# A front in another order and one query projection fewer in a hybrid attention layer

## The chip, the cores and the metric

The kernel runs on one core of a Trainium2 chip. The metric is the device time of one execution in microseconds, as the median of several runs; lower is better.

## The reference

The kernel computes one layer of a decoder trunk on x of 512 tokens by 1024 features, in float32:

```
h = rms_norm(x)
q,k,v (8 MoBA heads), q (8 NSA heads), kv (cmp,slc,win), gates = split(h @ w_in)
y_A = moba_attention(...)            # rms-normed q, k; relative bias table
y_B = nsa_attention(...)             # compressed, selected and window branch
x = x + (sigmoid(gA) * (y_A @ w_br_moba) + sigmoid(gB) * (y_B @ w_br_nsa)) @ w_o
x = x + (gelu(conv_a) * conv_b) @ w_down      # conv3 of rms_norm(x) @ w_up
x = x + sigmoid(x @ w_ple_gate) * (p @ w_ple)
```

With 512 tokens each of MoBA's selections and NSA's selected and window branches covers all past keys, so the kernel computes causal attention for them, and a small one over 31 compressed keys for the compressed branch.

## The kernel before

All weights and activations are split into a high part (rounded to fp32r) and a low part (the rest). Each product is three matmuls, high by high, high by low, low by high (`three`, L1400 to L1402). The token axis has NT = 4 tiles of 128, the depth axis KT = 8 tiles of 128. Five engines run programs written out by hand, with semaphores between them; the DMAs are issued by SP, a few at the start by ScalarE.

**The front.** SP loads x, the rows of constants, unit 0's weights in two halves and the first gate's weights. ScalarE and VectorE sum the squares of x. VectorE scales x (L1088) and splits unit 0's weights (L1057 high part, L1064 the low part of even depth tiles, GpSimd the low part of odd ones at L609, after it has built the bias table `rtab`, L601). TensorE turns x (L1417) and, after four of the eight depth tiles, the constants (L1408). ScalarE takes `hTh` out of PSUM (L846), VectorE `hTl` (L1097). Then TensorE projects unit 0, token tile by token tile with the depth inside, the first from the fifth `hTl` on, and runs gate 0. The vectors of unit 0 are turned (L1451) after GpSimd (L655, tiles 0 and 1) and VectorE (tiles 2 and 3) have copied them.

**The units.** A projection unit w brings the columns for one pair of heads. Units 1 to 4 have q, k and v of two MoBA heads (384 columns). Units 5 and 7 have q of two NSA heads and k and v of a group (384). Units 6 and 8 have q alone (128 columns). A unit's work after the projection is a sum of squares, `rstd`, `normalise` (L1150 on VectorE for token tiles 2 and 3, L639 on GpSimd for 0 and 1), the turning of its two or four vectors (`turn_vector`), and `vec_high`, `vec_low`, which take them into `QQ`, `Kh`, `Kl`.

**The attention** is a list of 104 steps, 8 for each of pairs 0 to 3 and 18 for each of pairs 4 to 7. A step takes the scores of one query tile of one head; steps 9 and 18 of the later pairs are those over the compressed keys. `PROJ`, `SPLIT`, `NORM` and `VEC` say at which step a piece of a later unit's work is done: unit 6 is projected in the first 8 steps of pair 4, unit 7 in the last 6 of pair 4 and the first 10 of pair 5, unit 8 in the first 8 of pair 6. Output gates are computed in between. Behind the attention come 184 chunks of weights for the branch products, `w_o`, the feed-forward part and the last gate.

## Time and profile before

| | us |
|---|---|
| median of 3 runs (1001.71 to 1003.32) | 1003.06 |
| the profiled execution, its own time | 1001.79 |
| its span in the trace | 1000.0 |
| TensorE busy | 914.0 |
| VectorE busy | 484.8 |
| ScalarE busy | 405.2 |
| GpSimd busy | 381.3 |

The trace is of one execution; times in it count from the start of its span. Matmuls are pipelined, so their records overlap: a matmul's duration is longer than the distance between two starts, and it is this distance that counts in a full stream. PE is TensorE, PEld its weight loads, DVE VectorE, ACT ScalarE, POOL GpSimd. The granted clock is 1.00 for 2.4 GHz and 0.50 for 1.2 GHz.

### The profile page before, as it was taken

To read this page: it belongs to the slowest core of one execution; us is meant where nothing else is said; L and a number is where in the kernel's file an instruction comes from. 1 tells how busy PE (TensorE), PEld (TensorE's weight loads), DVE (VectorE), ACT (ScalarE), POOL (GpSimd) and SP (SyncE) were. 2 spreads that over 40 slices of the span, in tenths; PEclk is the share of its full clock that TensorE was granted. 3 is DMA by queue.
4 is the path that set the end of the run, shared out by engine and by line. 5 is a ranking of instruction groups with operands and counts; after the bars stand their busy time and mean duration, and the time that the engine had idled before them with its cause. 6 is when DMAs were issued, how large, how long until landed. Compare 5 with 4: busy or idle time off the path is not lost.

```text
span 1000.0 us, 13463 instructions
## 1 busy us (share of the span) xinstructions
PE 914.0 (91%) x4621; PEld 779.4 (78%) x4621; DVE 484.8 (48%) x1179; ACT 405.2 (41%) x857; POOL 381.3 (38%) x364
## 2 busy tenths in 40 slices
PE   3998798787999799999989999999999999999988
PEld 2897688686878687877767778888888888888866
DVE  6516666767675767786441343344433343000032
ACT  3221454444454444554434344444444443232320
POOL 6333312312120301025544566444454445464540
PEclk9998899999999899999999999999999999999999
DMA  5655213214122111333554425333333333332222
GB/s 158 153 138 137 63 47 81 54 38 111 43 73 77 32 53 57 113 127 123 179 199 132 116 95 147 98 93 95 95 95 108 104 95 95 96 99 91 85 94 86
DMA packets 99046, 99.34 MB, mean 99 GB/s; under 512 B 16068, under 2 KB 73380, under 8 KB 98980
## 3 DMA queue, kind: packets, MB, share of 16 engines
q1 hardware_dynamic: 98927, 98.48, 33.7%
q8 instruction: 39, 0.64, 0.3%
q14 instruction: 27, 0.22, 0.1%
q10 hardware_dynamic: 53, 0.01, 0.0%
HBM read 87.58 MB, written 10.88 MB: 98 GB/s over the span
## 4 chain that ended last, share of the span: by engine, by line
PE 78%; DVE 13%; issue 4%; ACT 3%; DMA 1%; POOL 0%; SPq 0%; POOLq 0%; ACTq 0%; DVEq 0%
PE banks L1400 24%; PE banks L1402 23%; PE banks L1401 23%; DVE plain_arena L1150 2%; PE banks L1533 2%; DVE plain_arena L1178 1%; PE banks L1451 1%; DVE split_arena L1064 1%; DVE split_arena L1223 1%; PE banks L1516 1%; PE banks L1515 1%; PE banks L1475 1%; ACT split_arena L821 1%; DVE split_arena L1057 1%; DMA plain_arena<-in_x_dram 1%
## 5 line engine op out<-in xcount | busy, mean ns | idle before, releaser
L1400 PE MATMUL banks<-split_arena 128*128 128x512 f32 (+4 forms) x1256 | 479.1, 381 | 15.5 <-POOL split_arena L645 4.1
L1401 PE MATMUL banks<-split_arena 128*128 128x512 f32 (+4 forms) x1256 | 467.0, 372 | 0.0
L1402 PE MATMUL banks<-split_arena 128*128 128x512 f32 (+4 forms) x1256 | 466.9, 372 | 0.0
L645 POOL TENSOR_TENSOR split_arena<-plain_arena,split_arena 128x512 fp32r<-128x512 f32 x184 | 238.7, 1310 | 248.7 <-ACT split_arena L837 248.7
L1400 PEld LDWEIGHTS banks<-split_arena 128*128 128x128 f32 x1256 | 240.2, 191 | 59.3 <-issue 13.1
L1402 PEld LDWEIGHTS banks<-split_arena 128*128 128x128 f32 x1256 | 239.7, 191 | 36.2
L1401 PEld LDWEIGHTS banks<-split_arena 128*128 128x128 f32 x1256 | 240.4, 191 | 32.5
L837 ACT ACTIVATE split_arena<-plain_arena 128x512 fp32r<-128x512 f32 x184 | 113.3, 628 | 196.4 <-PE banks L1402 189.4
L809 ACT ACTIVATE plain_arena<-plain_arena 128x128 f32<-128x128 f32 (+1 forms) x96 | 53.9, 562 | 137.3 <-DVE plain_arena L1178 137.3
L1361 DVE SCALAR_TENSOR_TENSOR plain_arena<-banks,plain_arena 128x511 f32<-128x511 f32 x44 | 32.7, 743 | 135.4 <-ACT plain_arena L938 135.4
L613 POOL TENSOR_TENSOR split_arena<-plain_arena,split_arena 128x512 fp32r<-128x512 f32 x16 | 25.7, 1606 | 146.1 <-ACT split_arena L894 135.1
L609 POOL TENSOR_TENSOR split_arena<-plain_arena,split_arena 128x384 fp32r<-128x384 f32 (+2 forms) x36 | 36.3, 1019 | 106.4 <-ACT split_arena L752 92.9
L1178 DVE CUSTOM_DVE_ANT_0 plain_arena<-banks,plain_arena 128x128 f32<-128x128 f32 (+1 forms) x96 | 46.7, 486 | 43.0 <-PE banks L1516 42.5
L1223 DVE TENSOR_TENSOR split_arena<-banks,split_arena 128x128 fp32r<-128x128 f32 (+1 forms) x96 | 46.9, 489 | 36.1 <-ACT split_arena L821 35.9
L1533 PE MATMUL banks<-plain_arena 128*128 128x128 f32 x240 | 43.7, 281 | 9.7 <-DVE split_arena L1223 5.1
L1451 PE MATMUL banks<-plain_arena 128*128 128x128 f32 x128 | 22.2, 307 | 27.6 <-DVE plain_arena L1150 19.3
L1379 DVE TENSOR_TENSOR plain_arena<-banks,plain_arena 128x512 f32<-128x512 f32 x8 | 5.0, 683 | 86.4 <-PE banks L1402 86.4
L1451 PEld LDWEIGHTS banks<-plain_arena 128*128 128x128 f32 x128 | 16.2, 157 | 32.9 <-issue 21.5
L821 ACT ACTIVATE split_arena<-banks 128x128 fp32r<-128x128 f32 (+1 forms) x96 | 40.1, 418 | 2.2 <-PE banks L1533 1.2
L639 POOL TENSOR_TENSOR plain_arena<-plain_arena 128x256 f32<-128x256 f32 (+1 forms) x32 | 18.3, 603 | 58.6 <-DVE plain_arena L1048 29.8
L1533 PEld LDWEIGHTS banks<-plain_arena 128*128 128x128 f32 x240 | 28.9, 142 | 13.9 <-issue 12.4
L938 ACT ACTIVATE plain_arena<-banks,plain_arena 128x512 f32<-128x512 f32 x44 | 30.6, 777 | 22.3 <-PE banks L1402 22.3
(156 smaller groups left out, 843.2 us busy)
## 6 DMA issues: line engine op xcount, KB each, us to landing
plain_arena<-in_w_up_dram SPq DMA_DIRECT2D x88, 256.0 KB, 3.2
plain_arena<-in_w_down_dram SPq DMA_DIRECT2D x44, 256.0 KB, 2.6
plain_arena<-in_w_in_dram SPq DMA_DIRECT2D x18, 512.0 KB, 4.2
plain_arena<-in_w_in_dram SPq DMA_DIRECT2D x32, 192.0 KB, 3.6
plain_arena<-in_x_dram SPq DMA_DIRECT2D x8, 512.0 KB, 4.6
gates<-plain_arena SPq DMA_DIRECT2D x16, 256.0 KB, 2.3
plain_arena<-skew SPq DMA_DIRECT2D x16, 256.0 KB, 3.7
plain_arena<-in_w_in_dram SPq DMA_DIRECT2D x64, 64.0 KB, 2.1
```

Of the source, the lines that this page charges most:

```text
L609: pool.tensor_tensor(Wl[:, kt, 0:c], raw[:, kt, 0:c], Wh[:, kt, 0:c].bitcast(F32), ALU.subtract).then_inc(w_lo[1], 1)
L645: pool.tensor_tensor(W2l[:, c % RING, :], raw2[:, c % RING, :], W2h[:, c % RING, :].bitcast(F32), ALU.subtract).then_inc(w2_lo, 1)
L809: nc.scalar.activation(prob[:, t % 4, 0:nk], prob[:, t % 4, 0:nk], ACT.Exp, bias=mneg[:, t % 4:t % 4 + 1], scale=-1.0, accum_out=rsum[:, t ...
L821: nc.scalar.activation(PTh[:, s["u"] % 2, 0:i + 1, P * i:P * (i + 1)], PS[:, 4 + t % 2, 0:P * (i + 1)].rearrange("p (j q) -> p j q", j=i + ...
L837: nc.scalar.activation(W2h[:, c % RING, :], raw2[:, c % RING, :], ACT.Copy).then_inc(w2_hi, 1)
L1178: nc.vector.tensor_tensor_reduce(out=prob[:, t % 4, 0:nk], in0=PS[:, 2 + t % 2, 0:nk], in1=strip[:, n % 2, e, S - nk:S], scale=1.0, scalar ...
L1223: nc.vector.tensor_tensor(PTl[:, s["u"] % 2, 0:i + 1, P * i:P * (i + 1)], PS[:, 4 + t % 2, 0:P * (i + 1)].rearrange("p (j q) -> p j q", j= ...
L1400: nc.tensor.matmul(o, ah, bh, start=first, stop=False)
L1401: nc.tensor.matmul(o, ah, bl, start=False, stop=False)
L1402: return nc.tensor.matmul(o, al, bh, start=False, stop=last)
L1451: ins = nc.tensor.transpose(PS[:, vec_bank(w, x), P * tt:P * (tt + 1)], qn[:, tt, x, :], ident)
L1533: ins = nc.tensor.transpose(PS[:, 4 + t % 2, P * j:P * (j + 1)], prob[:, t % 4, P * j:P * (j + 1)], ident)
```

## The change

In the front, TensorE runs 20 matmuls of the constant `ones` by itself, turns the constants, runs 8 more of them, and only then turns x. ScalarE takes the high part of all of unit 0's weights before it copies the turned constants; GpSimd takes all low parts, under a semaphore of their own (`w0_lo`). VectorE no longer splits unit 0; it scales x in two halves of the features. GpSimd builds the bias table after unit 0's and gate 0's low parts instead of before. SP issues the second gate's load ahead of the skew table's spill. Unit 0 is projected with the depth outermost for two token tiles at a time, in four banks of PSUM. In the later units, unit 6 now brings the queries of pair 5 and of pair 7 (256 columns, four vectors), and unit 8 is gone; pair 7's queries stay in a third slot of `QQ`. The diff, cut to its core; the rest are places where 6 and 8 were excepted and uses of the new slot:

```diff
-        return 2 * P + 24 if w == 0 else (P if w in (6, 8) else CW)
+        return {0: 2 * P + 24, 6: 2 * P}.get(w, CW)
     def udmas(w):
         return {0: 0, 5: 3, 7: 3}.get(w, 1)
     def nvec(w):
-        return 2 if w in (6, 8) else 4
-
-    W_UNITS = 9
+        return 4
+
+    W_UNITS = 8
...
-        QQ = R[:, 24576:26624].rearrange("p (s e q) -> p s e q", s=2, e=2)
+        QQ = [R[:, o:o + 1024].rearrange("p (e q) -> p e q", e=2) for o in (24576, 25600, 37760)]
...
-            eng.wait_ge(w_lo[kt % 2], KT // 2 * w + kt // 2 + 1)
+            if w == 0:
+                eng.wait_ge(w0_lo, kt + 1)
+            else:
+                eng.wait_ge(w_lo[kt % 2], KT // 2 * (w - 1) + kt // 2 + 1)
...
+            if w == 0:
+                return (0, 1, 4, 5)[tt]
             return 6 if w <= 2 and tt % 2 and (w, tt) != (2, 3) else 0
...
+        def qslot(n):
+
+            return 2 if n == NPAIR - 1 else n % 2
+
         def vec_dst(w, x):
             n = w - 1
+            if w == 6:
+                return "q", qslot(5 if x < 2 else 7), x % 2
             if x < 2:
-                return "q", n % 2, x
+                return "q", qslot(n), x
             return ("k", n % 2, x - 2) if n < 4 else ("k", (n - 4) // 2, x - 2)
...
-                        sp.dma_start(raw[:, kt, 0:P], win[kt][:, C_NQ + n * P:C_NQ + (n + 1) * P]).then_inc(raw_in[kt], 16)
-                        if n % 2 == 0:
-
+                        if w == 6:
+                            src = win[kt][:, C_NQ:C_NQ + 512].rearrange("p (a b c) -> p a b c", a=2, b=2)[:, :, 1, :]
+                            sp.dma_start(raw[:, kt, 0:2 * P].rearrange("p (a c) -> p a c", a=2), src).then_inc(raw_in[kt], 16)
+                        else:
+                            sp.dma_start(raw[:, kt, 0:P], win[kt][:, C_NQ + n * P:C_NQ + (n + 1) * P]).then_inc(raw_in[kt], 16)
                             g = n // 2
...
+            load_gate_weights(1)
             sp.wait_ge(rtab_done, 1)
             for c0, part in ((0, rtab), (S, masked)):
                 width = part.shape[1]
                 sp.dma_start(skew_d[:, :, c0:c0 + width], part.unsqueeze(1).broadcast_to([16, NREP, width])).then_inc(skew_out, 16)
-            load_gate_weights(1)
...
-            pool.wait_ge(rbt_in, 16)
-            pool.wait_ge(pool_const, 12)
-
-            for b, (lo, hi) in enumerate(bucket_edges()):
-                ins = pool.tensor_scalar(rtab[:, S - hi:S - lo], rbt[:, b:b + 1].broadcast_to([16, hi - lo]), -1.0, None, ALU.mult)
-            ins.then_inc(rtab_done, 1)
-
             def split_unit(w, kts):
...
-            split_unit(0, range(KT))
+            for kt in range(KT):
+                pool.wait_ge(w_hi, kt + 1)
+                pool.tensor_tensor(Wl[:, kt, 0:ucols(0)], raw[:, kt, 0:ucols(0)], Wh[:, kt, 0:ucols(0)].bitcast(F32), ALU.subtract).then_inc(w0_lo, 1)
             split_gate(0)
+            pool.wait_ge(rbt_in, 16)
+            pool.wait_ge(pool_const, 12)
+
+            for b, (lo, hi) in enumerate(bucket_edges()):
+                ins = pool.tensor_scalar(rtab[:, S - hi:S - lo], rbt[:, b:b + 1].broadcast_to([16, hi - lo]), -1.0, None, ALU.mult)
+            ins.then_inc(rtab_done, 1)
             pool.wait_ge(cst_done, 1)
...
+            w_high(0, range(KT))
             act.wait_ge(cst_turned, 3)
             nc.scalar.activation(cst[:, 0:CONVW + P + 4], PS[:, 0, 0:CONVW + P + 4], ACT.Copy).then_inc(cst_done, 1)
...
-            for tt in range(NT):
-                nc.vector.tensor_scalar(xnat[:, tt, :], xnat[:, tt, :], st[:, 80 + tt:81 + tt], None, ALU.mult).then_inc(h_nat, 1)
-            split_unit(0, range(KT))
+            for half in range(2):
+                for tt in range(NT):
+                    part = xnat[:, tt, half * 512:(half + 1) * 512]
+                    nc.vector.tensor_scalar(part, part, st[:, 80 + tt:81 + tt], None, ALU.mult).then_inc(h_nat, 1)
             dve.wait_ge(cst_done, 1)
             dve.wait_ge(pool_const, 4)
-
-            for c in (GQ, GQ + 2):
-                link(nc.vector.tensor_scalar(cst[:, c:c + 1], cst[:, c:c + 1], -(DH ** -0.5), None, ALU.mult))
             for kt in range(KT):
                 dve.wait_ge(hT_hi, kt + 1)
                 nc.vector.scalar_tensor_tensor(out=hTl[:, kt, :], in0=PS[:, turn_bank(kt), :], scalar=cst[:, kt:kt + 1],
                                                in1=hTh[:, kt, :].bitcast(F32), op0=ALU.mult, op1=ALU.subtract).then_inc(hT_lo, 1)
+            for c in (GQ, GQ + 2):
+                link(nc.vector.tensor_scalar(cst[:, c:c + 1], cst[:, c:c + 1], -(DH ** -0.5), None, ALU.mult))
             gate_high(0)
...
-                if k == 4:
-                    rsqrt(rq[:, 0:16], ss[:, 0:16], 1.0 / DH, 16, done=rstd_done)
-                else:
-                    rsqrt(rq[:, 20:28], ss[:, 0:8], 1.0 / DH, 8)
-                    nc.vector.tensor_copy(rq[:, 0:16].rearrange("p (t v) -> p t v", t=NT)[:, :, 0:2],
-                                          rq[:, 20:28].rearrange("p (t v) -> p t v", t=NT)).then_inc(rstd_done, 1)
+                rsqrt(rq[:, 0:16], ss[:, 0:16], 1.0 / DH, 16, done=rstd_done)
...
-                    pe.wait_ge(h_nat, tt + 1)
+                    pe.wait_ge(h_nat, NT * (kt // 4) + tt + 1)
...
-                    if w == 0:
-                        pe.wait_ge(hT_lo, 5)
...
-            for kt in range(4):
+            def warm(count):
+
+                pe.wait_ge(pool_const, 4)
+                for _ in range(count):
+                    nc.tensor.matmul(PS[:, 7, 0:P], ones, ones, start=True, stop=True)
+
+            def project_first():
+
+                pe.wait_ge(cst_done, 1)
+                for pair in ((0, 1), (2, 3)):
+                    for kt in range(KT):
+                        wait_weights(pe, 0, kt)
+                        pe.wait_ge(hT_lo, kt + 1)
+                        for tt in pair:
+                            t_ = slice(P * tt, P * (tt + 1))
+                            ins = three(PS[:, proj_bank(0, tt), 0:ucols(0)], hTh[:, kt, t_], hTl[:, kt, t_], Wh[:, kt, 0:ucols(0)], Wl[:, kt, 0:ucols(0)],
+                                        kt == 0, kt == KT - 1)
+                            if kt == KT - 1:
+                                ins.then_inc(proj_filled, 1)
+                        if pair[1] == NT - 1 and kt < KT - 1:
+                            ins.then_inc(w_used, 1)
+
+            warm(20)
+            turn_consts()
+            warm(8)
+            for kt in range(KT):
                 turn_input(kt)
-            turn_consts()
-            for kt in range(4, KT):
-                turn_input(kt)
-            for tt in range(NT):
-                project(0, tt)
+            project_first()
             gate(0)
```

## Rows read from the trace of the kernel before

**Rows 1.** The page, part 4: the chain that ended last, by engine.
```profile
PE 78%; DVE 13%; issue 4%; ACT 3%; DMA 1%; POOL 0%; SPq 0%; POOLq 0%; ACTq 0%; DVEq 0%
```

**Rows 2.** Windows, TensorE: stretch, length, busy (x), granted clock, DMA share, GB/s.
```profile
13.00:14.00 1.00, 0.83 (x2) 1.00 0.84 188
14.00:15.00 1.00, 0.62 (x3) 1.00 0.04 8
...
22.00:23.00 1.00, 0.00 (x0) 0.84 0.00 0
...
29.00:30.00 1.00, 1.00 (x8) 0.75 1.06 291
```

**Rows 3.** The chain in order of time, first projection and pair 4: start, us, what.
```profile
25.75 0.60 PE banks L1400
...
27.05 0.23 PE banks L1401
...
35.12 0.13 PE banks L1401
...
251.87 0.11 PE banks L1401
...
254.86 0.12 PE banks L1402
```

**Rows 4.** Timeline of VectorE: start, us, instruction, forms, count.
```profile
14.80 0.51 DVE L1057 CAST split_arena<-plain_arena 128x280 fp32r<-128x280 f32 x2
...
16.38 3.18 DVE L1057 CAST split_arena<-plain_arena 128x280 fp32r<-128x280 f32 x2
...
22.31 5.36 DVE L1097 SCALAR_TENSOR_TENSOR split_arena<-banks,plain_arena,split_arena 128x512 fp32r<-128x512 f32 x8
...
273.71 0.89 DVE L1150 TENSOR_TENSOR plain_arena<-plain_arena 128x128 f32<-128x128 f32 x4
...
341.22 3.31 DVE L1150 TENSOR_TENSOR plain_arena<-plain_arena 128x256 f32<-128x256 f32 x4
```

**Rows 5.** Timeline of GpSimd in the front, columns as before.
```profile
9.10 9.51 POOL L601 TENSOR_SCALAR plain_arena<-plain_arena 16x1 f32<-16x1 f32 x32 [4.34 <-DMA plain_arena<-in_rel_bias_dram]
18.58 2.34 POOL L609 TENSOR_TENSOR split_arena<-plain_arena,split_arena 128x280 fp32r<-128x280 f32 x3
...
28.34 1.79 POOL L613 TENSOR_TENSOR split_arena<-plain_arena,split_arena 128x512 fp32r<-128x512 f32 x1 [5.69 <-DVE split_arena L1075]
31.35 0.74 POOL L655 COPY plain_arena<-plain_arena 128x256 f32<-128x256 f32 x2 [1.22 <-ACT plain_arena L747]
```

**Rows 6.** Windows between compressed-key steps: busy (x) of PE, PEld, DVE, ACT, POOL; clock; DMA.
```profile
326.72:361.50 34.78, 28.30 (x157) 23.61 (x156) 26.29 (x84) 17.61 (x48) 10.75 (x14) 0.90 0.11 32
361.50:389.43 27.93, 27.93 (x193) 25.11 (x193) 16.09 (x61) 12.29 (x36) 1.79 (x1) 1.00 0.26 75
389.43:415.69 26.26, 22.50 (x135) 18.95 (x133) 21.65 (x78) 12.62 (x32) 4.17 (x6) 1.00 0.13 41
415.69:435.65 19.96, 19.48 (x110) 16.10 (x109) 15.22 (x58) 10.04 (x28) 1.78 (x1) 1.00 0.64 206
435.65:458.34 22.69, 19.71 (x114) 16.21 (x112) 18.65 (x58) 14.28 (x36) 9.43 (x7) 1.00 0.25 87
```

**Rows 7.** Groups by form, ScalarE: xcount | busy us, mean ns | idle before.
```profile
L752 ACT ACTIVATE split_arena<-plain_arena 128x384 fp32r<-128x384 f32 x32 | 14.2, 511 | 0.0
...
L846 ACT ACTIVATE split_arena<-banks,plain_arena 128x512 fp32r<-128x512 f32 x8 | 4.9, 693 | 1.9 <-PE banks L1417 1.9
```

**Rows 8.** Timeline of TensorE, after the first gate and in the feed-forward part.
```profile
45.28 1.03 PE L1451 MATMUL banks<-plain_arena 128*128 128x128 f32 x8
...
48.31 0.42 PE L1400 MATMUL banks<-split_arena 128*128 128x384 f32 x1
...
578.60 1.16 PE L1639 MATMUL banks<-plain_arena 128*128 128x128 f32 x8 [1.58 <-DVE plain_arena L1345]
```

**Rows 9.** Line L1417, window 13 to 20.2 us: duration ns min/median/max, first and last start.
```profile
L1417 PEld LDWEIGHTS banks<-plain_arena x24: 141/230/231, 13.0 to 19.5; 128*128 128x128 f32 x24
```

More of the change, by code:

```diff
@@ L288, in layer @@
         cst_done = sem("cst_done")
+        w0_lo = sem("w0_lo")
         w_hi, w_lo = sem("w_hi"), [sem("w_lo_even"), sem("w_lo_odd")]
@@ L685, in _ @@
                     normalise(NORM[t])
-                if t in VALUES and VALUES[t] not in (6, 8):
+                if t in VALUES and VALUES[t] != 6:
                     v_low(VALUES[t])
@@ L744, in take_proj @@
                     act.wait_ge(norm_done, w)
-                    if w - 1 not in (6, 8):
-                        act.wait_ge(v_lo, min(w - 1, 5) if w - 1 < 7 else 6)
+                    if w < 7:
+                        act.wait_ge(v_lo, w - 1)
                 nc.scalar.activation(qkv[:, tt, 0:ucols(w)], PS[:, proj_bank(w, tt), 0:ucols(w)], ACT.Copy).then_inc(qkv_done, 1)
@@ L902, in _ @@
                     w_high(*SPLIT[t])
-                if t in VALUES and VALUES[t] not in (6, 8):
+                if t in VALUES and VALUES[t] != 6:
                     v_high(VALUES[t])
@@ L1514, in scores @@
                     nk = P * (i + 1)
[L1515 to L1516 removed]
+                    nc.tensor.matmul(o[:, 0:nk], QQ[qslot(n)][:, e, P * i:P * (i + 1)], Kh[:, ks, ke, 0:nk], start=True, stop=False)
+                    ins = nc.tensor.matmul(o[:, 0:nk], QQ[qslot(n)][:, e, P * i:P * (i + 1)], Kl[:, ks, ke, 0:nk], start=False, stop=True)
                 ins.then_inc(score, 1)
```

18 lines of the change are left out of this document (8 added, 10 removed).

## The prediction

> **What bounds the kernel now.** I read the page's chain first: TensorE holds 78% of it and VectorE 13% [rows 1]. So time is won in two ways only: by taking matmuls out of TensorE's stream, or by closing stretches in which it waits. The windows show such a stretch at the start: the transfers are over by 14 us (share 0.84 in 13:14, 0.04 in 14:15) [rows 2], yet the first projection begins at 25.75 us [rows 3]. VectorE's timeline shows what lies between: unit 0's weights are split from 14.80 us on, with one pair of casts that took 3.18 us where the same pair took 0.51 before, and only at 22.31 us does it come to `hTl` (L1097), for which the projection waits [rows 4]. GpSimd was building the bias table then, from 9.10 us for 9.51 [rows 5]. Last, the windows from one compressed-key step (the 9th and the 18th of each pair of heads 4 to 7) to the next show what a projection unit costs inside the attention [rows 6].
>
> **The front, part by part.** *Weights of unit 0* go from VectorE to ScalarE and GpSimd. A 384-column cast takes ScalarE 0.51 us [rows 7]; I take 0.4 for 280 columns. The second half of the weights lands between 12 and 14 us, I take 13.0, so the last four casts end at 14.6 us. The copy of the turned constants now stands behind them in ScalarE's order, some 0.4 us: 15.0. That is the new wait, and all of `hTh` and `hTl` are queued behind it; the constants themselves are turned earlier. *x* is scaled in halves: the whole is done at 14.8 us as before, the first half over a microsecond earlier, so turning x lies beside ScalarE's casts. The first `hTh` takes 0.7 us [rows 7]: 15.7. Then `hTl` paces with 5.36/8 = 0.67 us [rows 4]. TensorE's last turn (kt 7) needs the second `hTl`, at 17.1 us, and takes some 0.6 us: the projection starts at 17.7 us instead of 25.75.
>
> *Depth-outermost.* A 280-column matmul advances by 0.23 us at the low clock level and 0.13 at the high one [rows 3] (0.127, from the end point below). A depth step of two tiles is six of them, 0.76 us, longer than the 0.67 between two `hTl`: TensorE isn't starved. GpSimd's low parts of the weights take 2.34/3 = 0.78 us each [rows 5], kt 7 done by 19 us, wanted at 23. The 96 matmuls take 12.2 us and end at 29.9. Before, the gate followed the last one 24 x 0.228 = 5.5 us ahead of 45.28 [rows 8], at 39.8. Gain 9.9 us. Of this 1.6 is clock: before, the first 3.7 us of the projection ran at 1.2 GHz (15 matmuls x 0.106).
>
> *Constant matmuls.* 28 of them run from about 1.5 us, when TensorE has nothing else before 13 us. Their nearest row, the products with `ones` at 578.60 us, has 8 passes for 4 products in 1.16 us [rows 8]: 0.25 us each at 2.4 GHz, at most twice that at 1.2. So 20 are over at 6.5 to 11.5 us and the 8 behind the constants take 2 to 4 us, over before 15. Their cost is nothing: they lie beside the loads and ScalarE's casts, and if that cover were gone it would be the 2 to 4 us of the last 8. What they buy is the high level. The granted clock fell within 22:23, about 3 us after TensorE had gone idle, and rose within 29:30 [rows 2]. In the new order I find no idle stretch over 1.5 us ahead of the projection and price it at the high level.
>
> The Trainium skill (TensorE: Matmul & The Clock Gate, Part 4: PE-mode transpose) says that work in the transpose mode doesn't count towards opening the full clock. By it the constant matmuls would be forgotten while x is turned, and the projection would start at 1.2 GHz, 1.6 to 2.9 us more. The trace of before speaks against it: from 13.0 us TensorE did almost nothing but transposes, and their weight loads went from 231 to 141 ns within them [rows 9].
>
> *GpSimd's bias table* moves behind unit 0's weights and the gate's. The gate's high part is there at about 22.2 us (`hTl` ends at 21.1, then two small instructions and one cast), its low part takes 1.79, then the table 9.51: 33.5 us. Four copies follow, 0.74 for two: 35.0 us [rows 5]. Turning unit 0's vectors waits for them, and TensorE comes to it when the gate ends, 29.9 + 5.5 = 35.4 us. That is a cover of 0.4 us. Behind the copies GpSimd splits the odd weights of unit 1, 4 x 0.78 x 384/280 = 4.3 us: 39.3, wanted at 35.4 + 3.0 [rows 8] + 3.6 = 42.0. VectorE's casts for unit 1 fall beside the table this time, as unit 0's did before. I charge 1.0 us for this corner; the bounds are 0 and 4. On SP the spill of the skew table waits for the table, with the loads of unit 1 and of gate 1 ahead of it; the strips that read it are wanted tens of microseconds later. Front: -9.9 + 1.0 = **-8.9 us**. The later waits of the front hang on TensorE's own progress and move along.
>
> **The merged unit.** Units 6 and 8 are 96 matmuls of 128 columns each. Such a matmul advances by 0.11 us (piece at 251.87), and one of 256 columns by 0.12 (254.86) [rows 3]. Halving the count saves TensorE 96 x 0.11 = 10.6 us. What of it reaches the path is read from [rows 6], where like steps stand beside each other. Nine steps with unit 8's projection take 27.93 us, the same nine a pair later without one 19.96: -7.97 (not 10.6, since the softmax chain shows through). The nine with unit 8's normalisation and two vectors take 26.26, without 22.69: -3.57. Against it, pair 4 gets two more vectors to turn, eight transposes, 1.0 us [rows 8], and a normalisation 256 wide. On VectorE four 128-wide instructions took 0.89 us, four 256-wide ones beside GpSimd 3.31 [rows 4]. Unit 6 has no values for GpSimd to split, so only the first of the four meet it: I take 2.2 us, +1.3. With 0.2 for wider matmuls and copies: -7.97 - 3.57 + 1.0 + 1.3 + 0.2 = **-9.0 us**. Bounds: with the transposes alone -10.3. If the merged unit behaves like unit 7, the window 326.72:361.50 applies: 34.78 less 2.1 (two steps of its projection, 12 matmuls at 0.17) less 22.69 = 10.0 for a four-vector unit against 3.57 for a two-vector one, 6.4 more: -5.1. I stay near the first end, since unit 7's values are what unit 6 lacks. The third query slot takes a wait away and adds none; eight dropped SP issues, four ScalarE copies and one VectorE rsqrt chain are in the windows already.
>
> **Sum.** 1001.79 (the profiled run, whose span is 1000.0) - 8.9 - 9.0 = 983.9: **984 us**. The median shown is 1.3 above that run, so 985 would be as fair.
>
> **Rivals.** (a) *The four-vector stall.* Merging gives 5.1: 1001.8 - 8.9 - 5.1 = 988. For it: in unit 7's window the clock fell to a mean of 0.90 [rows 6]. Against: no value split. (b) *The front meets GpSimd.* Table, copies and odd weights are 3 us later than summed, weights or clock cost another 1: 1001.8 - 4.9 - 9.0 = 988. For it: the 0.4 us of cover and the 3.18 us pair [rows 4]. Against: most of VectorE's work then is ahead of need. The Trainium skill has a rule that would sharpen it (SBUF — State Buffer, Who interferes with whom): VectorE's casts and GpSimd's instructions block each other for whole instructions rather than slow each other a little. (c) *Both*: 992. (d) *Better than summed*: no collision, no widening, one fall of the clock fewer: 979 to 981. (e) *Slower than before*: the table, now ahead of unit 0's copies, holds TensorE back so long that 17.9 us are gone. It decides from the point where it takes 9.5 + 0.4 + 1.0 + 17.9 = 29 us; at 32 the kernel is at 1005. The worst collision seen is 3.2 us for a pair, so this needs six such. (f) *Nothing happens in front*, since x or weights bind: 1001.8 - 9.0 = 993. Against: VectorE had x and all weights in hand by 16.38 us at the latest, without a wait [rows 4].
>
> **Numbers.** The forecast (981 to 987) 0.45, (a) 0.17, (b) 0.17, (c) 0.06, (d) 0.08, (f) 0.03, within 0.2% 0.01, (e) 0.03. The range goes from 979 to 992 and holds the first five. Within 0.2% (2 us) is about what a measurement of this kernel can't tell from no change. Faster 0.96, same 0.01, slower 0.03.
>
> **What would show it.** Right: the first 280-column matmul at 17 to 18.5 us with 0.127 between starts; the gate's first at 29 to 31; no wait of the vectors' turning for L655; all of the attention some 9 us earlier at its start; the nine steps after pair 5 in 20 to 21 us, not 27.93; pair 4's stretch 2 to 3 us longer. Wrong: a projection that starts at 0.23 us spacing, VectorE casts of over 1 us between 24 and 34 us with TensorE waiting for them, or a pair 4 stretch over 5 us longer.

## The result, and the profile after

The changed kernel takes 994.37 us (median of 4 runs, 993.43 to 994.84) against 1003.19 us (median of 4 runs, 1001.71 to 1006.77): a ratio of 0.9903, 95% interval 0.9886 to 0.992. It is faster by 8.8 us, where 17.9 were summed. The profiled execution took 993.43 us, its span is 991.6 us.

First the page of the changed kernel, part 4, the chain by engine. It answers to [rows 1]: TensorE has the same share, VectorE one per cent less.

```profile
PE 78%; DVE 12%; issue 4%; ACT 4%; DMA 1%; POOL 0%; SPq 0%; POOLq 0%; ACTq 0%; DVEq 0%
```

TensorE's timeline in the front (start, us, instruction, forms, count, idle before). L1577 are the constant matmuls, L1428 turns x, the 280-column matmuls are the first projection, the first 512-column one is the gate, L1460 turns the vectors of unit 0.

```profile
1.53 7.61 PE L1577 MATMUL banks<-plain_arena 128*128 128x128 f32 x40 [1.53 <-POOL plain_arena L603]
9.99 0.56 PE L1419 MATMUL banks<-plain_arena 98*128 98x98 f32 x3 [0.85 <-DMA plain_arena<-in_conv_w_dram]
10.49 2.05 PE L1577 MATMUL banks<-plain_arena 128*128 128x128 f32 x16
...
17.01 5.05 PE L1428 MATMUL banks<-plain_arena 128*128 128x128 f32 x29 [0.58 <-DVE plain_arena L1106]
21.82 0.38 PE L1411 MATMUL banks<-split_arena 128*128 128x280 f32 x1
...
34.04 0.29 PE L1413 MATMUL banks<-split_arena 128*128 128x280 f32 x1
34.17 0.39 PE L1411 MATMUL banks<-split_arena 128*128 128x512 f32 x1
...
39.63 1.04 PE L1460 MATMUL banks<-plain_arena 128*128 128x128 f32 x8
43.77 1.26 PE L1460 MATMUL banks<-plain_arena 128*128 128x128 f32 x8 [3.10 <-DVE plain_arena L1130]
```

The projection starts at 21.82 us instead of 25.75 [rows 3], and runs through at 0.13 us from one matmul to the next. But it was to start at 17.7. TensorE turns x late, and its idle time names L1106, VectorE's scaling of x. Behind the gate it waits 3.10 us for L1130. VectorE's timeline says why in both places:

```profile
11.57 0.16 DVE L1062 TENSOR_TENSOR plain_arena<-plain_arena 128x4 f32<-128x4 f32 x1
11.76 0.71 DVE L1063 SCALAR_TENSOR_TENSOR plain_arena<-plain_arena 128x4 f32<-128x4 f32 x1
12.51 0.70 DVE L1064 SCALAR_TENSOR_TENSOR plain_arena<-plain_arena 128x4 f32<-128x4 f32 x1
13.24 6.35 DVE L1106 TENSOR_SCALAR plain_arena<-plain_arena 128x512 f32<-128x512 f32 x8
19.51 5.35 DVE L1111 SCALAR_TENSOR_TENSOR split_arena<-banks,plain_arena,split_arena 128x512 fp32r<-128x512 f32 x8
...
34.42 4.84 DVE L1121 COPY plain_arena<-plain_arena 128x256 f32<-128x256 f32 x4 [1.56 <-ACT plain_arena L762]
...
274.84 2.90 DVE L1161 TENSOR_TENSOR plain_arena<-plain_arena 128x256 f32<-128x256 f32 x4
```

And GpSimd's, to be laid beside it:

```profile
11.67 6.84 POOL L658 TENSOR_TENSOR split_arena<-plain_arena,split_arena 128x280 fp32r<-128x280 f32 x8 [6.91 <-ACT split_arena L767]
25.91 1.80 POOL L620 TENSOR_TENSOR split_arena<-plain_arena,split_arena 128x512 fp32r<-128x512 f32 x1 [7.40 <-DVE split_arena L1091]
27.68 7.94 POOL L664 TENSOR_SCALAR plain_arena<-plain_arena 16x1 f32<-16x1 f32 x32
35.58 1.52 POOL L670 COPY plain_arena<-plain_arena 128x256 f32<-128x256 f32 x4
```

GpSimd begins to subtract unit 0's low parts at 11.67 us. From that moment an instruction of VectorE on 128x4 values takes 0.71 us instead of 0.16, and the scaling of x takes 6.35 us. The four copies of the vectors (34.42 to 39.26 us) lie beside the end of the bias table, GpSimd's own copies and its first weights of unit 1, and take 4.84 us.

Windows over the stretches that stand in [rows 2], and one behind: busy (x) of the engines, clock, DMA. The clock falls at the end of 17:18, behind TensorE's short waits for x, stands at 0.50 in 18:21 and is back at 1.00 in 22:23. So x is turned mostly at the low level, and the projection that begins at 21.82 us is not. It falls again in 45:46, behind the wait for L1130.

```profile
17.00:18.00 1.00, 0.99 (x8) 1.00 (x9) 1.00 (x2) 0.56 (x1) 1.00 (x2) 0.92 0.00 0
18.00:21.00 3.00, 3.00 (x16) 2.89 (x15) 3.00 (x6) 2.65 (x5) 0.51 (x1) 0.50 0.00 0
22.00:23.00 1.00, 1.00 (x10) 1.00 (x9) 1.00 (x3) 0.93 (x2) 0.00 (x0) 1.00 0.00 0
29.00:30.00 1.00, 1.00 (x10) 1.00 (x9) 0.02 (x1) 0.00 (x0) 1.00 (x7) 1.00 1.21 291
45.00:46.00 1.00, 1.00 (x6) 1.00 (x5) 0.92 (x2) 0.98 (x3) 0.00 (x0) 0.57 0.06 16
```

Windows from one compressed-key step to the next, as in [rows 6]; the first row is pair 4's stretch, which ends unit 6 (31.14 us before).

```profile
268.73:303.10 34.37, 30.43 (x169) 26.87 (x168) 28.94 (x85) 17.87 (x44) 10.04 (x10) 0.90 0.11 32
...
365.78:385.76 19.98, 19.49 (x109) 15.97 (x108) 15.35 (x58) 10.04 (x28) 1.79 (x1) 1.00 0.36 104
385.76:407.33 21.57, 19.61 (x116) 16.50 (x114) 16.49 (x58) 11.47 (x30) 3.19 (x2) 1.00 0.16 50
```

27.93 us have become 19.98, and 26.26 have become 21.57. So what unit 8 cost is gone, and pair 4's stretch is 3.2 us longer. What came in its place shows best in a table of leads: how much earlier than before an attention step starts (the start of VectorE's bias instruction on the scores; steps counted from 0 over the whole attention). "From x" is the lead at step 0 counted from the end of ScalarE's last sum of squares instead of from the start of the span; why, is said below the table. "Spread" is the lowest and highest run.

| kernel | lead at step 0 | from x | 26 | 50 | 103 | span | median (spread), runs | ratio, 95% interval |
|---|---|---|---|---|---|---|---|---|
| before: start of the step | 103.96 | 94.23 | 217.42 | 301.61 | 458.34 | 1000.0 | | |
| changed | +1.96 | +1.97 | +1.63 | -4.06 | +8.31 | 991.6 | 994.37 (993.43 to 994.84), 4 | 0.9903, 0.9886 to 0.992 |
| 1 merge only | -0.20 | +0.46 | -0.08 | -7.29 | +5.57 | 995.1 | 997.18 (995.42 to 998.41), 6 | 0.9931, 0.9909 to 0.9952 |
| 2 front only | +0.90 | +2.15 | -0.16 | -0.16 | -0.69 | 1003.6 | 1002.92 (998.42 to 1005.64), 12 | 0.9981, 0.9962 to 1.0 |
| 3 GpSimd after x | +5.64 | +5.64 | +4.87 | -0.81 | +11.01 | 988.2 | 990.8 (989.85 to 992.72), 6 | 0.9868, 0.9847 to 0.989 |
| 4 table late | +5.96 | +6.05 | +4.64 | -1.04 | +11.88 | 992.0 | 992.78 (991.25 to 993.77), 5 | 0.9891, 0.9872 to 0.9909 |
| 5 both | +8.64 | +9.45 | +7.82 | +2.07 | +14.46 | 985.3 | 987.05 (986.91 to 987.41), 4 | 0.983, 0.9805 to 0.9855 |
| 6 changed, no constant matmuls | +0.95 | +1.95 | -0.09 | -5.77 | +7.12 | 993.3 | 995.78 (994.39 to 999.3), 6 | 0.9928, 0.9908 to 0.9948 |
| 7 = 5 + gate waits | +8.71 | +9.49 | +7.14 | +2.51 | +15.02 | 984.4 | 986.69 (983.61 to 987.4), 5 | 0.9828, 0.9808 to 0.9848 |
| 8 = 5 + halves | +9.11 | +10.11 | +7.66 | -0.08 | +12.25 | 987.3 | 989.04 (987.89 to 990.4), 5 | 0.9854, 0.9833 to 0.9875 |
| 9 = 7 + unit 6 on GpSimd | +9.21 | +10.21 | +7.66 | +5.21 | +18.27 | 983.4 | 984.2 (983.95 to 985.21), 4 | 0.9802, 0.9781 to 0.9823 |
| 10 = 7, depth innermost | +7.50 | +8.55 | +7.44 | +1.28 | +13.73 | 987.5 | 989.29 (988.3 to 990.22), 4 | 0.9851, 0.9825 to 0.9876 |
| 11 = 9 + unit 7 on GpSimd | +9.25 | +10.29 | +8.05 | +6.16 | +18.11 | 983.5 | 987.69 (985.58 to 989.59), 5 | 0.9831, 0.9808 to 0.9854 |
| 12 = 9, no constant matmuls | +8.71 | +8.77 | +8.60 | +6.04 | +18.41 | 982.3 | 986.12 (984.13 to 989.33), 5 | 0.9825, 0.98 to 0.9849 |

Each lead comes from one profiled execution. One thing in it is no edit's doing: the last rows of x land early in some of them and about a microsecond later in others. ScalarE's last sum of squares waits for them, as here in the kernel before and in run 9:

```profile
8.58 1.06 ACT L734 ACTIVATE split_arena<-plain_arena 128x1024 fp32r<-128x1024 f32 x1 [1.04 <-DMA plain_arena<-in_x_dram]
```

```profile
9.58 1.06 ACT L754 ACTIVATE split_arena<-plain_arena 128x1024 fp32r<-128x1024 f32 x1 [2.05 <-DMA plain_arena<-in_x_dram]
```

Its result is out at 9.73 to 9.82 us before, in the changed kernel and in runs 3, 4 and 12, and at 10.39 to 10.98 in the others; the column "from x" takes this out. What is left of chance shows in runs 5, 7, 8, 9 and 11, whose programs are the same up to step 0: +9.45 to +10.29. A single difference below about 0.8 us at step 0 shows nothing by itself.

Read the row "changed" from left to right. The front is worth 1.96 us where attention starts. Between steps 26 and 50 (the splits, projection, normalisation and vectors of the merged unit) 5.69 us are lost; from 50 to 103, where unit 8 used to be, 12.37 are won.

### The profile page after: what moved, and what is told of

It reads as the page before. It is cut to its first block, busy times and chain, and to the rows that moved or that the text cites. A ratio compares the mean times of both kernels' runs of the same rounds, so it can differ in the third digit from the quotient of the medians.

```text
span 991.6 us, 13260 instructions
## 1 busy us (share of the span) xinstructions
PE 913.8 (92%) x4581; PEld 779.1 (79%) x4581; DVE 485.4 (49%) x1145; ACT 405.8 (41%) x849; POOL 381.8 (38%) x360
## 4 chain that ended last, share of the span: by engine, by line
PE 78%; DVE 12%; issue 4%; ACT 4%; DMA 1%; POOL 0%; SPq 0%; POOLq 0%; ACTq 0%; DVEq 0%
PE banks L1411 24%; PE banks L1413 23%; PE banks L1412 23%; DVE plain_arena L1161 2%; PE banks L1542 2%; PE banks L1460 1%; DVE plain_arena L1189 1%; DVE split_arena L1080 1%; DVE split_arena L1234 1%; PE banks L1525 1%; PE banks L1524 1%; ACT split_arena L836 1%; PE banks L1484 1%; DMA plain_arena<-in_x_dram 1%; ACT plain_arena L824 1%
## 5 line engine op out<-in xcount | busy, mean ns | idle before, releaser
L1411 PE MATMUL banks<-split_arena 128*128 128x512 f32 (+4 forms) x1224 | 471.3, 385 | 15.7 <-POOL split_arena L652 4.1
L1413 PE MATMUL banks<-split_arena 128*128 128x512 f32 (+4 forms) x1224 | 459.1, 375 | 0.0
L1412 PE MATMUL banks<-split_arena 128*128 128x512 f32 (+4 forms) x1224 | 458.6, 375 | 0.0
L1411 PEld LDWEIGHTS banks<-split_arena 128*128 128x128 f32 x1224 | 234.6, 192 | 58.8 <-issue 12.4
L1413 PEld LDWEIGHTS banks<-split_arena 128*128 128x128 f32 x1224 | 233.4, 191 | 36.3
L1412 PEld LDWEIGHTS banks<-split_arena 128*128 128x128 f32 x1224 | 234.5, 192 | 32.7
L616 POOL TENSOR_TENSOR split_arena<-plain_arena,split_arena 128x384 fp32r<-128x384 f32 (+1 forms) x28 | 31.3, 1127 | 100.7 <-ACT split_arena L767 91.8
L1460 PE MATMUL banks<-plain_arena 128*128 128x128 f32 x128 | 22.6, 311 | 29.0 <-DVE plain_arena L1161 19.8
L1460 PEld LDWEIGHTS banks<-plain_arena 128*128 128x128 f32 x128 | 16.5, 159 | 34.4 <-issue 22.0
L762 ACT ACTIVATE plain_arena<-banks 128x384 f32<-128x384 f32 (+2 forms) x32 | 14.8, 463 | 51.6 <-PE banks L1413 42.0
```

The costliest lines, as they stand in the source:

```text
L1411: nc.tensor.matmul(o, ah, bh, start=first, stop=False)
L1412: nc.tensor.matmul(o, ah, bl, start=False, stop=False)
L1413: return nc.tensor.matmul(o, al, bh, start=False, stop=last)
L1460: ins = nc.tensor.transpose(PS[:, vec_bank(w, x), P * tt:P * (tt + 1)], qn[:, tt, x, :], ident)
```

## The experiments

### 1 and 2: one part alone

Run 1 is the kernel before with the merge; run 2 has the new front and units 6 and 8 apart.

> The kernel before with the merged query units alone. If the two halves of the change add up as the two traces say (first compressed-key step of pair 4 0.8 us later and that of pair 7 8.3 us earlier, 1.6 us ahead just before unit 6 begins to cost), this run is 6 to 7 us faster than before, and its nine steps after pair 5 take about 20 us. If the merge paid only because the front had relieved VectorE and GpSimd, it is less than 4 us faster.

> The changed front with units 6 and 8 apart. By the traces the front is worth 1.5 to 2.5 us: the first projection begins at 21.8 us and not at 25.75, but the first attention step only 2 us earlier. The rival is that the front is worth nothing (within 0.5 us), since the lead of 2 us shrinks again before pair 4.

The ratios say -6.9 us and -1.9 us, together 8.8, where the changed kernel's ratio says -9.7. Run 2's interval reaches 1.0 and its runs spread over 7 us, so its total alone doesn't show a gain; its front, counted from x, starts attention 2.15 us earlier, like the changed kernel's 1.97. Nothing here points to the two parts meeting, and both fell short of the forecast, the front by more. From step 50 to 103 the merge alone wins 12.86; from step 26 to 50 it loses 7.21, of which 1.6 stand at steps 30 to 32 behind a fall of the clock that the changed kernel does not have there.

### 3, 4 and 5: GpSimd out of VectorE's way

```diff
 # 3: GpSimd's low parts of unit 0 start when x is scaled
+pool.wait_ge(h_nat, 2 * NT)
 for kt in range(KT):
     pool.wait_ge(w_hi, kt + 1)
     pool.tensor_tensor(Wl[:, kt, ...], ...)
 # 4: the bias table moves from before the copies of unit 0's vectors to behind
 #    GpSimd's second share of the compressed inputs; the stores of the skew
 #    table on SP go behind load_gate_weights(2)
 # 5: 3 and 4
```

> The changed kernel, with GpSimd's low parts of unit 0 started only after VectorE has scaled x. Theory: these subtractions held up VectorE (eight half tiles in 6.35 us, the last two rsqrt instructions 0.7 us instead of 0.16). Then here the eight take 2.8 to 3.3 us, the projection begins at 17.5 to 18.5 us and ends at 30 to 31. Rival: the halved instructions or ScalarE's casts slow VectorE; then the eight still take over 5 us. At the attention's start I expect at most 1 to 2 us of it, if the bias table's place is the next limit: VectorE's copies and casts for unit 1 stay beside the table.

> The changed kernel with one move: GpSimd builds the bias table (8 us) only after it has subtracted the second set of compressed inputs, so not beside VectorE's four copies of the first unit's vectors; the stores that need the table go behind the gate weights in SP's queue. GpSimd's subtractions stay where the change put them, beside VectorE's scaling of x. Theory (the table beside the copies is the second loss of the front, and independent of the first): the four copies fall from 4.84 to below 2 us, TensorE's stall at the vectors of unit 0 from 3.37 to about 1.2 us, the clock does not fall at 45 us, the first attention step comes 3.5 to 4 us earlier, and the time is 990 to 991.5 us. Rival (the table costs wherever it stands, beside later work of VectorE): the stall moves behind the copies and the time stays at 993.5 to 994.5 us.

> As the run before, and the bias table built after the compressed keys' inputs, where GpSimd is idle (its small input lies in another place, and the skew table is spilled later). Theory: with the table away VectorE's four copies take 1.7 us instead of 4.84, its part of turning unit 0 is not late (2.1 us), the clock does not fall at 45 us (1.7 us), and the 4 us of the run before come through: attention starts 6 to 8 us earlier than in the changed kernel, 987 us. Rival: another wait in the stretch from 48 to 100 us absorbs it, under 3 us faster than the changed kernel.

Run 3, VectorE's timeline:

```profile
11.75 0.16 DVE L1064 SCALAR_TENSOR_TENSOR plain_arena<-plain_arena 128x4 f32<-128x4 f32 x1
12.14 3.26 DVE L1107 TENSOR_SCALAR plain_arena<-plain_arena 128x512 f32<-128x512 f32 x8
15.78 5.36 DVE L1112 SCALAR_TENSOR_TENSOR split_arena<-banks,plain_arena,split_arena 128x512 fp32r<-128x512 f32 x8 [0.38 <-ACT split_arena L863]
...
30.78 4.80 DVE L1122 COPY plain_arena<-plain_arena 128x256 f32<-128x256 f32 x4 [1.39 <-ACT plain_arena L763]
```

The small instructions are back at 0.16 us, x is scaled in 3.26 us, `hTl` starts at 15.78 us (predicted: 15.7), and TensorE's first 280-column matmul at 17.66 (predicted: 17.7). The copies still lie beside the end of the table and what follows it (4.80). Lead at step 0: +3.68 over the changed kernel; at most 1 to 2 us had been expected.

Run 4, VectorE's copies and TensorE's turning of the vectors, one line from either timeline:

```profile
34.11 0.90 DVE L1121 COPY plain_arena<-plain_arena 128x256 f32<-128x256 f32 x4 [1.14 <-ACT plain_arena L762]
```

```profile
41.33 1.26 PE L1460 MATMUL banks<-plain_arena 128*128 128x128 f32 x8 [0.97 <-DVE plain_arena L1130]
```

4.84 us have become 0.90, TensorE's wait 0.97 instead of 3.10, and the clock does not fall at 45 us. Lead at step 0: +4.00 over the changed kernel, as expected, and +3.57 at step 103. The time, though, fell by less than 2 us, and the rival "it costs wherever it stands" seems to have won. It has not: the lead is lost behind the attention, where nothing was changed. Windows of run 4:

```profile
504.00:512.00 8.00, 6.57 (x21) 5.59 (x22) 4.97 (x7) 2.30 (x4) 3.36 (x2) 0.57 0.63 202
562.00:570.00 8.00, 7.74 (x28) 6.59 (x29) 4.13 (x17) 1.60 (x3) 1.28 (x1) 0.57 0.52 172
961.00:969.00 8.00, 6.50 (x16) 5.14 (x17) 4.46 (x6) 0.02 (x1) 1.26 (x1) 0.57 0.70 244
```

The same places in the changed kernel:

```profile
508.00:516.00 8.00, 7.00 (x28) 5.97 (x29) 4.87 (x6) 3.73 (x7) 4.15 (x3) 0.79 0.64 207
566.00:574.00 8.00, 6.43 (x32) 4.85 (x30) 5.15 (x17) 3.21 (x6) 1.79 (x2) 1.00 0.46 151
962.00:970.00 8.00, 6.40 (x22) 5.20 (x23) 4.56 (x6) 0.11 (x1) 1.26 (x1) 0.79 0.76 244
```

At each of them TensorE has a short wait and then runs for a while at 1.2 GHz; a mean of 0.57 over 8 us is 6.9 us at that level, 0.79 is 3.4, 1.00 none. Run 4 has some 14 us more of it in these three windows, and its span is 3.9 us longer than its lead at step 103 says (11.88 against 8.0). The program behind step 103 is the same in both, so small edits are judged by the lead at the next marks rather than by the total. That the low-clock time is all of the 3.9 us is not shown.

Run 5 has both: +8.64 at step 0. Counted from x the gains over the changed kernel are 3.67 and 4.08 alone and 7.48 together, so they add to within 0.3 us. **The front was forecast to be worth 8.9 us; without the two meetings it was worth 8.6, or 9.45 counted from x.** The copies take 1.19 us.

### 6 and 12: what the constant matmuls bring

```diff
-warm(20)
 turn_consts()
-warm(8)
```

> The changed kernel without the 28 constant matmuls (20 ahead of the turning of the constants, 8 behind it); nothing else is changed. Theory (the turning of x raises the clock by itself and the granted clock of the first projection does not come from the constant matmuls): the first projection still advances by about 0.13 us per matmul from its second half on at the latest, the loss is 0 to 1.5 us, 994 to 996 us. Rival (the constant matmuls carry the clock over the first projection): its 96 matmuls run at 0.22 us instead of 0.127 us each for most of its length, the first gate starts 5 to 9 us later than 34.2 us, and the time is 999 to 1003 us.

> The version of 984.2 us without the 28 constant matmuls. Theory (the clock rises from the turning of x alone about 3 to 7 us after it begins, as in the run without them on the changed kernel): now that the projection starts at 18.3 instead of 21.8 us, its first matmuls fall into the low level, until about 21 us, and the loss at the start of attention is 1 to 2 us, 985 to 986.5 us. Rival (with the projection earlier the constant matmuls carry it): the low level lasts over half of the projection, 5 us or more lost. Rival of the other side: no loss, 984 us.

By the plain leads they are worth 1.01 us at step 0 on the changed kernel and 0.50 on the best version. Both are distorted by x, which landed a microsecond late in run 6 and early in run 12. Counted from x the changed kernel loses nothing without them (1.97 against 1.95), and the best version 1.44 us (10.21 against 8.77). That is more than chance: from the start of x's scaling to the first 280-column matmul it is 6.58 us in run 12, and 5.04 to 5.31 in the five runs that have the same front and the constant matmuls. TensorE's timeline of run 12:

```profile
12.84 6.19 PE L1433 MATMUL banks<-plain_arena 128*128 128x128 f32 x32 [2.00 <-DVE plain_arena L1111]
18.79 0.38 PE L1416 MATMUL banks<-split_arena 128*128 128x280 f32 x1
```

and of run 9, which has them:

```profile
13.77 4.75 PE L1433 MATMUL banks<-plain_arena 128*128 128x128 f32 x32 [0.42 <-DVE plain_arena L1111]
18.28 0.37 PE L1416 MATMUL banks<-split_arena 128*128 128x280 f32 x1
```

Run 12 begins to turn x 0.93 us earlier and starts the projection 0.51 us later: that is the 1.44 us. It turns x at the low level at first (6.19 us instead of 4.75); its weight loads for that take 0.23 us up to 17.4 us and 0.14 behind it, though the profile's row of the granted clock says 1.00 from 12.8 us on. The projection runs at the full clock: the turning itself has raised it. So the first theory stands, and the loss of 1.4 us is the expected 1 to 2. On the changed kernel nothing is lost: x is turned mostly at the low level there with the constant matmuls too (0.50 in 18:21). The gain does not last: at step 26 run 12 is 0.94 us ahead of run 9 by the plain lead, and at step 103 0.14. Its total spreads over 5 us and settles nothing by itself.

### 7, 8, 9 and 11: the merged unit

In run 5 the 5.75 us lost between steps 26 and 50 lie in four places, by the same leads: 1.71 while unit 6's weights are split (steps 26 to 30), 0.74 with its projection (30 to 41), 2.31 at its normalisation (41 to 42), 0.99 with its vectors.

```diff
 # 7: GpSimd's gate subtraction at unit 6 starts when VectorE has normalised
+if t > n6 and not gated: gated.append(j); pool.wait_ge(norm_dve, 7)
 split_gate(j + 1)
 # 8: VectorE normalises two of unit 6's vectors, and the others a step later
-if t - 1 in NORM: normalise(NORM[t - 1])
+if t - 1 in NORM: normalise(6, 0, 2) if NORM[t - 1] == 6 else normalise(NORM[t - 1])
+if t - 2 in NORM and NORM[t - 2] == 6: normalise(6, 2, 4)
 # 9: unit 6's low parts all on GpSimd (11: unit 7's too)
-if kt % 2:
+if kt % 2 or w == 6:
```

> The version with both GpSimd moves (987.05 us) and one wait more: at unit 6 GpSimd's subtraction for the gate weights (1.53 us) starts only when VectorE has normalised its half of unit 6. Theory (VectorE's 2.90 us for four 128x256 instructions is its meeting with GpSimd's subtraction): they take 1.5 to 2.0 us, TensorE's stall of 4.27 us at 267.9 us falls to 3.1 to 3.4 us, and the time is 986 us. Rival (256 columns cost what they cost): 2.90 us and 4.27 us stay, and the time is 987 us.

> The version with both GpSimd moves (987.05 us), and VectorE normalises the two vectors for pair 5 of unit 6 where it now does all four, and the two for pair 7 one attention step later (four instructions of 128x128 twice instead of four of 128x256 once). Theory (the merge's extra stall is VectorE doing twice the work in one place with TensorE waiting behind it): the first half takes 0.9 to 1.5 us, TensorE's stall of 4.27 us at 267.9 us falls to about 2 to 2.8 us as before the change, little of it comes back a step later, and the time is 985 to 986 us. Rival (the work only moves to the next step, where TensorE waits for it too): one stall of 2.3 us and a new one of 1.5 to 2 us, and the time is 987 us.

VectorE's timeline of run 7, then of run 8, at the normalisation:

```profile
269.34 1.83 DVE L1166 TENSOR_TENSOR plain_arena<-plain_arena 128x256 f32<-128x256 f32 x4
```

```profile
270.28 2.37 DVE L1161 TENSOR_TENSOR plain_arena<-plain_arena 128x128 f32<-128x128 f32 x4
```

In run 7 the four instructions take 1.83 us instead of 2.90 once GpSimd's subtraction is out of the way; TensorE loses 1.24 us there instead of 2.31. Run 8 has half the work in the first place and still takes 2.37 us, where the same form took 0.89 before the change [rows 4]. GpSimd is what differs: before, its own half of the normalisation was over (272.17 + 1.47 = 273.64 us) when VectorE's began at 273.71. One of run 8's four, of 128x128, bears most of it:

```profile
271.10 1.35 DVE L1161 TENSOR_TENSOR plain_arena<-plain_arena 128x128 f32<-128x128 f32 x1
```

Run 7's last three, clear of GpSimd, take 1.08 us, so four of 128x256 would take about 1.4 (an estimate from that). Then the meetings cost the same at either width, 2.37 - 0.89 = 1.5 and 2.90 - 1.4 = 1.5, and the width about 0.5. Run 8 pays for the second half too: by the leads it loses 0.5 us less than run 5 at the normalisation and 1.0 more in the steps behind. It ends 2 us behind run 5, but most of that is not the edit's: 1.5 us are lost between steps 30 and 32, before the normalisation, where the clock fell (a mean of 0.66 in 231:236) and run 5's did not.

> The version with both GpSimd moves and the gate's wait at unit 6 (986.69 us), and the low parts of unit 6's weights are all subtracted by GpSimd, where VectorE takes every other one (0.86 us of VectorE in each of four steps beside GpSimd's 0.72, where 128 columns took 0.29 before the change). Theory (attention steps 27 to 30 lengthen by 0.4 to 0.6 us each because VectorE's and ScalarE's splits of unit 6 are twice as wide): with VectorE's part gone the lead over the kernel before falls between steps 26 and 30 by 0 to 0.6 us instead of 1.7, and the time is 985.0 to 986.0 us. Rival (ScalarE's 0.72 instead of 0.51 us sets the steps, or GpSimd's longer work slows VectorE as much): the lead still falls by 1.4 us or more, and the time is 986.5 to 987 us or above.

The splits, VectorE's timeline of run 5 with two of its four halves:

```profile
223.45 0.87 DVE L1081 TENSOR_TENSOR split_arena<-plain_arena,split_arena 128x256 fp32r<-128x256 f32 x1
...
227.81 0.86 DVE L1081 TENSOR_TENSOR split_arena<-plain_arena,split_arena 128x256 fp32r<-128x256 f32 x1
```

In run 9 these lines are gone, GpSimd does all eight; the first four:

```profile
221.63 2.98 POOL L616 TENSOR_TENSOR split_arena<-plain_arena,split_arena 128x256 fp32r<-128x256 f32 x4
```

From step 26 to 30 the lead now rises by 0.40 us where run 7 loses 1.73: the whole cost of the splits in these steps was VectorE's share. Both are measured in the same stretch, so this is shown. Part of it is again a meeting: in run 5 GpSimd's own subtraction ran from 227.66 to 228.38 us, and VectorE's of 227.81 ended only at 228.67. With 984.2 us run 9 is the fastest here, 10 us below the changed kernel. That it lies 0.2 from the forecast is chance, since it got there by edits that the forecast did not have.

> The version of 984.2 us (both GpSimd moves, the gate's wait at unit 6, unit 6's low parts on GpSimd), with unit 7's low parts on GpSimd alone too (384 columns, 1.14 us each, two in a step). Theory (VectorE leads the chain of every step in which weights are split, and GpSimd has time): the lead rises by 0.5 to 1.5 us over the steps in which unit 7 is split, 983 to 984 us. Rival (in these steps TensorE has its projection to do and waits for nobody): the lead does not change, 984 to 984.5 us; or GpSimd is late for the projection of unit 7 and the time is 985 us or more.

The lead at step 50 rose by 0.95 us, inside what was expected, but nothing of it is left at step 103, and the median is 3.5 us higher, with no run as fast as run 9's slowest. A gain is not shown. The expectation's reason for a slower kernel, GpSimd late for unit 7's projection, doesn't fit a lead that had risen by step 50; where the 3.5 us are lost stays open.

### 10: depth innermost

```diff
-for pair in ((0, 1), (2, 3)):
+for pair in ((0,), (1,), (2,), (3,)):
     for kt in range(KT):
```

> The version with both GpSimd moves and the gate's wait at unit 6 (986.69 us), with the first unit's projection turned back from depth-outermost in two pairs of token tiles to one token tile after the other; banks and everything else stay. Theory (worked from the trace: a pair of depth tile takes TensorE 0.8 us and VectorE delivers one hTl in 0.67 us, so depth-outermost never waits, while one token tile alone takes 0.4 us for each depth tile and is paced by the 0.67 us): the projection ends 1 us later, the first attention step 1 us later, 987.5 to 988 us. Rival (something behind the projection sets the start of attention in any case): no change, 986.3 to 987 us. Rival of the other side (the order is the main gain of the front): 3 us later or more.

TensorE's timeline of run 10 has gaps in the first token tile, where it waits for `hTl`:

```profile
20.73 0.29 PE L1418 MATMUL banks<-split_arena 128*128 128x280 f32 x1
21.11 0.40 PE L1416 MATMUL banks<-split_arena 128*128 128x280 f32 x1
...
21.47 0.29 PE L1418 MATMUL banks<-split_arena 128*128 128x280 f32 x1
```

Between the start of the last matmul of one depth step and the first of the next lie 0.38 us instead of 0.13, and a depth step takes 0.74 us (20.73 to 21.47). The loss at step 0 is 1.21 us, or 0.94 counted from x, near the 1 us worked out. The total lost 2.6, but this is not the order's price: at step 26 the lead is again run 7's (7.44 against 7.14), and between steps 30 and 32 1.5 us are lost where run 10's clock fell (a mean of 0.66 in 233:238) and run 7's did not. So the new order is worth about 1 us where attention starts, and a lasting gain is not shown.

## Why the prediction was wrong

**The sign was right and the size was half: two meetings of VectorE with GpSimd and the price of the wider splits were missing from the sum.** The first step that failed is the sentence "the whole is done at 14.8 us as before": the scaling of x. It is done at 19.6. The prediction took this duration over from the kernel before and did not ask what GpSimd would be doing beside it. Before the change GpSimd was building its table there, and VectorE's small instructions took 0.16 us and the whole scaling 2.74 beside it; now it is eight wide subtractions, which the change itself brings forward to 11.67 us. All of the chain behind it (`hTh`, `hTl`, the projection) is the sum's, 3.8 to 4.3 us late: the first `hTl` 19.51 for 15.7, the first matmul 21.82 for 17.7, the gate 34.17 for 29.9. Run 3 takes that one meeting away and gets 15.78 and 17.66.

**The corner of table, copies and odd weights** was charged 1.0 us with bounds of 0 and 4. It costs 4.00 (run 4), the upper end: the second step that failed. GpSimd itself was in time: the table took 7.94 us and not 9.51, its copies were done at 37.1, before TensorE came at 39.6. Late was VectorE: the prediction found its casts for unit 1 ahead of need and did not look at the four copies, with casts and the copies of the compressed inputs (L1130) queued behind them. Rival (b) named the engines and the 4 us, but put the delay on GpSimd. Together the two account for the front: 9.9 - 3.7 - 4.0 = 2.2 us, measured 1.96.

**Depth-outermost, ScalarE's casts, the clock.** The projection was never starved, and its matmuls advanced by 0.129 us (12.22 us over 95), 0.127 predicted. The casts were done at 14.4 us (14.6 predicted), the copied constants at 14.7 (15.0). The constant matmuls cost nothing, but they did not do what they were priced for. TensorE waited 1.81 us for x where the prediction found "no idle stretch over 1.5 us", and the granted clock was 0.50 from 18 to 21 us; it was back before the projection began at 21.82, but not for the prediction's reason, since the projection has the high level without the constant matmuls too (runs 6 and 12). So the price held by luck. Where x comes in time they save some 1.4 us of its turning. With both meetings out of the way the front was worth 8.64 us in run 5 against 8.9, or 9.45 counted from x.

**The merge.** Its removals were summed at 7.97 + 3.57 = 11.5 us; 12.4 were won. The vectors (1.0) cost 0.99. Normalisation was put at +1.3 and cost 2.3: the term assumed that one of the four instructions lies beside GpSimd, and the gate's subtraction of 1.53 us met a second one, for about 1.1 us (2.90 against run 7's 1.83). "0.2 for wider matmuls and copies" is the worst mis-sized and the third step that failed: 1.7 for the splits and 0.7 for the projection, 2.4 in all. The prediction looked at TensorE for the wider weights, where they are nearly free, and not at VectorE, where a subtraction took 0.57 us more in each of the steps (0.86 against 0.29). Only some 0.1 of that is width, since clear of GpSimd an instruction of 256 columns takes about 0.4 (run 7); the rest, by this estimate, is the wait for GpSimd's own subtraction. So the merge gives 12.4 - 5.7 = 6.7 us, between the forecast of 9.0 and rival (a)'s 5.1.

**The sum as measured:** 1.96 for the front at step 0, less 0.33 up to step 26, less 5.69, plus 12.37, plus 0.1 behind the attention: 8.4 us of span. Rival (c), (a) and (b) together at 992, is the nearest in mechanism. Rival (f) at 993 is nearer in number, but x and the weights did not bind: the projection starts 3.9 us earlier, and what was lost was lost to GpSimd.

**The rules.** The rule of the Trainium skill (SBUF — State Buffer, Who interferes with whom) that was quoted behind rival (b) is borne out: by it a copy, cast or scaling of VectorE and a GpSimd instruction can lock each other out for whole instructions, and an instruction of VectorE with two inputs from SBUF meets GpSimd's reads. The trace agrees: 0.16 to 0.71 us on 128x4 values is not a share of a port but the wait for one GpSimd instruction (6.84/8 = 0.86 us). The rule alone would not have priced this front, though: beside the table the same small instructions took 0.16 us before the change. It also says that outside the two-port modes an instruction with at most one such input doesn't meet GpSimd: L1112 with its input from the banks took 5.36 us for eight beside GpSimd's subtractions, and 5.36 before [rows 4]. The rule of the Trainium skill against the transposes (TensorE: Matmul & The Clock Gate, Part 4) isn't borne out: in run 12 turning x (`nc.tensor.transpose`, 32 MATMUL records in f32) was nearly all that TensorE did, its weight loads went from 0.23 to 0.14 us within that, and the projection behind it ran at the full clock.

**The table is not one kind of work.** Read one by one, its 32 instructions are 31 short ones of 1 to 14 columns and a last one of 399. GpSimd before the change, four of the short ones beside the scaling of x, and the last one:

```profile
12.14 2.15 POOL L601 TENSOR_SCALAR plain_arena<-plain_arena 16x3 f32<-16x3 f32 x4
17.39 1.21 POOL L601 TENSOR_SCALAR plain_arena<-plain_arena 16x399 f32<-16x399 f32 x1
```

In the changed kernel a short one with VectorE idle, and the last one:

```profile
31.80 0.22 POOL L664 TENSOR_SCALAR plain_arena<-plain_arena 16x4 f32<-16x4 f32 x1
34.41 1.21 POOL L664 TENSOR_SCALAR plain_arena<-plain_arena 16x399 f32<-16x399 f32 x1
```

Beside the scaling of x it was GpSimd that was held up: 2.15 us for four instructions that take some 0.2 each. This is most of the 1.57 us by which the table is shorter now. The wide one is what VectorE meets: its cast of 16.38 us ended at 18.77, just behind 17.39 + 1.21 = 18.60, and the first of its four copies now starts at 34.42 and takes 1.35 us.

**Left open:** why that cast had not gone ahead of the short instructions before the wide one, and what decides how long TensorE stays at the low level behind a wait.

## What to carry to other kernels

Work moved to GpSimd to relieve VectorE is only relief when the two are not busy in the same microseconds: lay both timelines beside each other at the new place before summing, look at every instruction that VectorE has there, and count up to one GpSimd instruction of waiting for each. A duration taken beside another kind of GpSimd work doesn't carry over (2.74 us beside the table's short instructions, 6.35 beside the subtractions). When a unit is widened, price every engine that touches its columns, since the matmul may be the one that is nearly free. And read a gain at marks in the timeline as well as from the total, and count from the landing of the first input: here 4 us won in the front were gone from the total behind stretches at the low clock in a part that the edit did not touch, and a microsecond of x landing late hid what the constant matmuls do.

## What the hardware showed that was not expected

- Halving the width hardly helped: beside GpSimd, four 128x128 multiplications of VectorE took 2.37 us, and four of 128x256 took 2.90; clear of it, four of 128x128 took 0.89. The meetings cost some 1.5 us at either width.
- The wait goes both ways: beside VectorE's scaling of x, four small instructions of GpSimd took 2.15 us, and one of them takes 0.22 with VectorE idle.
- Giving VectorE's 0.86 us subtraction to GpSimd made GpSimd no slower: four took it 2.98 us (0.75 each), where one took 0.72 to 0.91 beside VectorE.
- Behind waits that look alike TensorE ran at 1.2 GHz for very different times (none, 3.4 and 6.9 us in the windows of experiment 4), and behind step 103 run 4 lost 3.9 us of its lead, with 14 us more at that level than the changed kernel.
